# Where the last cached values, the forget rows and the first input weights are kept, in a hybrid decoder step on one core

## The reference, cut to what matters

```python
z = xn @ w_in                  # columns: conv B | C | x | q | k | v | forget logits | two merge gates
y_conv = (cb * dwconv3(cc * cx)) @ w_up_conv
# forgetting attention, 8 heads of 64; d is the running sum of log f
prompt: softmax(q.k / 8 + d_q - d_k, causal) @ v
sample: softmax over [4096 cached positions, own new positions], per sequence
    k_past = cache_k[page_table]; v_past = cache_v[page_table]; rev = sums of the cached log f
mixed = sigmoid(gA) * y_conv + sigmoid(gB) * (attn @ w_up_attn)
h = h + mixed @ w_mix_out
```

## Time and profile before

| what | value |
|---|---|
| runs | 2205.54, 2205.38, 2199.3 us; median 2205.38 us |
| profiled execution | 2202.59 us, its span in the trace 2200.9 us, mean granted TensorE clock 0.966 |
| busy: TensorE, its weight loads, VectorE, ScalarE, GpSimd | 2024.1, 1206.5, 717.2, 488.5, 260.9 us |
| chain that ended last | PE 83%, DMA 4%, DVE 4%, issue 3% |
| moved by DMA | 458.69 MB, mean 208 GB/s |

### The profile page before, as it was taken

One profiled execution on the slowest core, in us unless ns is written; L12 is line 12 of the kernel. 1 busy time (PEld: TensorE's weight loads), 2 busy tenths in 40 slices (PEclk: granted clock), 3 DMA queues, 4 the chain that ended last, 5 costly groups with the idle time before them and its releaser, 6 DMA issues.

```text
span 2200.9 us, 34422 instructions
## 1 busy us (share of the span) xinstructions
PE 2024.1 (92%) x12894; PEld 1206.5 (55%) x12894; DVE 717.2 (33%) x1652; ACT 488.5 (22%) x1058; POOL 260.9 (12%) x402
## 2 busy tenths in 40 slices
PE   7899998999969999999999989898599999999994
PEld 5677765666644665788888446654333333333331
DVE  5221223666630142333333550633511111111115
ACT  3212222544420100111110111423022222222223
POOL 1001222222223000000000000000011111111120
PEclk9999998999988999999999999999699999999997
DMA  7546777888886111310111120403799999999976
GB/s 281 179 151 230 244 268 264 273 283 275 271 283 238 48 48 52 102 48 10 58 48 63 64 79 1 144 20 145 275 374 382 383 372 371 376 374 373 370 275 242
DMA packets 205070, 458.69 MB, mean 208 GB/s; under 512 B 18721, under 2 KB 44338, under 8 KB 204778
## 3 DMA queue, kind: packets, MB, share of 16 engines
q1 hardware_dynamic: 172330, 357.96, 46.2%
q0 software_dynamic: 32576, 98.53, 13.0%
HBM read 432.51 MB, written 32.17 MB: 211 GB/s over the span
## 4 chain that ended last, share of the span: by engine, by line
PE 83%; DMA 4%; DVE 4%; issue 3%; ACT 2%; SPq 2%; DVEq 1%; POOLq 0%; ACTq 0%; POOL 0%
PE ps L1575 10%; PE ps L1057 10%; PE ps L1322 9%; PE ps L1606 5%; PE ps L1329 5%; PE ps L1586 5%; PE ps L1188 5%; PE ps L1085 5%; PE ps L1359 4%; PE ps L1615 3%; PE ps L1100 2%; PE ps L1448 2%; PE ps L1224 2%; PE ps L1199 2%; PE ps L1137 2%
## 5 line engine op out<-in xcount | busy, mean ns | idle before, releaser
L1057 PE MATMUL ps<-xnT,ring 128*128 128x352 f32 x768 | 231.3, 462 | 1.8 <-ACT xnT L727 1.8
L1575 PE MATMUL ps<-gu,xgT 128*64 128x512 f32 x1024 | 229.7, 601 | 0.9 <-ACT xgT L1936 0.9
L1057 PEld LDWEIGHTS ps<-xnT,ring 128*128 128x128 f32 x768 | 145.6, 191 | 88.8 <-issue 8.3
L2860 POOL DMA_DIRECT2D vpage<-in_cache_v x256 | 137.9, 539 | 439.9 <-issue 431.2
L1188 PE MATMUL ps<-consts,kraw 128*128 128x128 f32 x1024 | 142.6, 284 | 29.3 <-DMA kraw<-in_cache_k 17.8
L1188 PEld LDWEIGHTS ps<-consts,kraw 128*128 128x128 f32 x1024 | 115.9, 144 | 62.4 <-issue 32.0
L2211 DVE COPY kt<-ps 128x512 f32<-128x512 f32 x128 | 88.3, 691 | 183.9 <-PE ps L1188 183.2
L1575 PEld LDWEIGHTS ps<-gu,xgT 128*64 128x64 f32 x1024 | 71.3, 138 | 134.1 <-issue 131.0
L1606 PE MATMUL ps<-wd,hidT_a 128*64 128x512 f32 x512 | 116.9, 598 | 19.7 <-ACT hidT_a L1946 12.5
L2751 DVE TENSOR_TENSOR sig_a<-ps,sig_a 128x256 f32<-128x256 f32 x32 | 13.6, 425 | 326.4 <-ACT sig_a L1940 326.4
L1586 PE MATMUL ps<-gu,xgT 128*32 128x512 f32 x1024 | 115.8, 592 | 0.0
(11 more groups left out here) (429 smaller groups left out, 2862.9 us busy)
## 6 DMA issues: line engine op xcount, KB each, us to landing
kraw<-in_cache_k SPq DMA_DIRECT2D x256, 256.0 KB, 3.6
vpage<-in_cache_v POOLq DMA_DIRECT2D x256, 256.0 KB, 4.7
gu<-in_w_expert_gate SPq DMA_DIRECT2D x32, 2048.0 KB, 20.3
gu<-in_w_expert_up SPq DMA_DIRECT2D x32, 2048.0 KB, 24.8
wd<-in_w_expert_down SPq DMA_DIRECT2D x31, 2048.0 KB, 9.2
ring<-in_w_in SPq DMA_DIRECT2D x8, 1024.0 KB, 7.2
yy<-y_d SPq DMA_DIRECT2D x16, 512.0 KB, 10.1
early<-in_w_in SPq DMA_DIRECT2D x6, 1024.0 KB, 10.7
```

The costliest lines, as they stand in the source:

```text
L1057: last = nc.tensor.matmul(bank(R.bank(*tag))[:, 0:NC_], slot[:, k, f * P:(f + 1) * P], xnT[:, k, cols_of(n)], start=k == 0, stop=k == KD - 1)
L1575: last = nc.tensor.matmul(bank(0)[h * BA:(h + 1) * BA, :].rearrange("p (x n) -> p x n", x=2), src[:, k, 0:BA], weight[:, k, :, h * DE // 2 ...
L2860: pool.dma_start(vpage[n % VS][:, p, :], t["cache_v"][ds(page, 1)].rearrange("a s d -> (a s) d")).then_inc(v_in[n % VS], 16)
```

## The change

Five edits, all in the mixer's stretch but the last:

1. Values of units 54 to 63 rotate through four places: the two before and the two of `kraw`. Unit 54 waits for the last keys' turning (`kt` 62) and 55 for `kt` 63; from 56 on a unit waits for the unit that had its place (52, 53, 54, ...).
2. All loops run over 74 slots instead of 64. Units 54 to 63 are weighed one a slot, one after another, and the twelve products of `cc` stand behind them, with nothing between. The last sequence's probabilities are turned in slot 65.
3. The two pairs of places of `negk` are exchanged. Pair 0 now goes to ring place 0 and is sent in SP's step 27, after the second column block of k; pair 1 goes to the area of `xnT`, sent in step 35. Pairs 2 and 3 stay in steps 41 and 49 (`slot_after`), and the prompt's units, written by a new formula, fall into the same slots as before.
4. `cc` goes to ring place 1 and is sent first, once the scores of unit 63 are made; then `xnT`, then `cx` to place 0. All later names take the other place. `xo` (place 0) is sent ahead of `xq` (place 1), which now waits for the last product of `w_mix_out`.
5. Semaphores are merged (`wfz` with `early_k`, `halo` with `mem`), and VectorE drains before it masks a sequence's sum.

```diff
@@ -58,7 +58,7 @@
-RING_ORDER = ["cc", "cx", "cb", "xk", "xv", "g0", "g1", "g2", "g3", "mo0", "mo1", "xq", "xo"]
+RING = {"cc": 1, "cx": 0, "cb": 1, "xk": 0, "xv": 1, "g0": 0, "g1": 1, "g2": 0, "g3": 1, "mo0": 0, "mo1": 1, "xo": 0, "xq": 1}
@@ -232,7 +232,7 @@
-        negk = [[at(f"negk{d}{p}", [P, SEQ], (a_norm + 6 * 4096 if d == 0 else a_ring) + p * 4096) for p in range(2)]
+        negk = [[at(f"negk{d}{p}", [P, SEQ], (a_norm + 6 * 4096 if d == 1 else a_ring) + p * 4096) for p in range(2)]
@@ -249,8 +249,8 @@
-        VS = 2
-        vpage = [at("vpage0", [P, 4, DA], a_mem), at("vpage1", [P, 4, DA], w + 5 * 4096)]
+        VS, MORE_VS = 2, DB * SU - SU - 2
+        vpage = [at("vpage0", [P, 4, DA], a_mem), at("vpage1", [P, 4, DA], w + 5 * 4096)] + kraw
@@ -482,9 +482,11 @@
+        END = PROMPT0 + PROMPT_SLOTS
+
...
-            return [(n - PROMPT0, 0), (n - PROMPT0, 1)] if PROMPT0 <= n < PROMPT0 + NU else []
+            return [(x // 2, x % 2) for x in range(2 * NU) if PROMPT0 + x * PROMPT_SLOTS // (2 * NU) == n]
@@ -529,14 +532,10 @@
-            if n > SU and n % SU == 1:
+            if SU < n < NSU + SU and n % SU == 1:
                 add_probs(n // SU - 1)
-        R.add("dve", "so", DB - 2, banks=(6,))
-        add_probs(DB - 1)
...
-            if x == SU - 1:
-                R.add("dve", "so", DB - 1, banks=(6,))
@@ -773,40 +772,44 @@
-            return ring[RING_ORDER.index(f"g{f // 2}") % 2].rearrange("p k (x n) -> p k x n", x=2)[:, :, :, f % 2 * P:(f % 2 + 1) * P]
+            return ring[RING[f"g{f // 2}"]].rearrange("p k (x n) -> p k x n", x=2)[:, :, :, f % 2 * P:(f % 2 + 1) * P]
...
-        LOADS = {"cc": (w3(t["w_in"], O_CC), None), "cx": (w3(t["w_in"], O_CX), ("sq", NSU - 1)),
+        LOADS = {"cc": (w3(t["w_in"], O_CC), ("sq", NSU - 1)), "cx": (w3(t["w_in"], O_CX), ("po", NU - 1)),
...
-                 "xq": (w3(t["w_xq"], 0), ("m6", 0)), "xo": (w3(t["w_xo"], 0, D), ("m3", PAIRS - 1))}
+                 "xo": (w3(t["w_xo"], 0, D), ("m6", 0)), "xq": (w3(t["w_xq"], 0), ("m3", PAIRS - 1))}
...
-            n = RING_ORDER.index(name)
+            n = RING[name]
...
-            dst = ring[n % 2] if src.shape[1] == KD else ring_xo
+            dst = ring[n] if src.shape[1] == KD else ring_xo
...
-                    sp.dma_start(dst[:, :, x * 256:(x + 1) * 256], src[:, :, x]).then_inc(ring_in[n % 2], 16)
+                    sp.dma_start(dst[:, :, x * 256:(x + 1) * 256], src[:, :, x]).then_inc(ring_in[n], 16)
                 else:
-                    sp.dma_start(dst, src).then_inc(ring_in[n % 2], 16)
+                    sp.dma_start(dst, src).then_inc(ring_in[n], 16)
...
-            n = RING_ORDER.index(name)
-            pe.wait_ge(ring_in[n % 2], 16 * sum(ring_parts(x) for x in RING_ORDER[n % 2:n + 1:2]))
-            return ring[n % 2]
+            n, loaded = RING[name], 0
+            for other in RING:
+                loaded += ring_parts(other) if RING[other] == n else 0
+                if other == name:
+                    break
+            pe.wait_ge(ring_in[n], 16 * loaded)
+            return ring[n]
@@ -820,6 +823,14 @@
+
+        def value_place(n):
+
+            return n % VS if n < MORE_VS else (n - MORE_VS + VS) % 4
+
+        def values_in(n):
+
+            return sum(value_place(m) == value_place(n) for m in range(n))
@@ -866,7 +877,7 @@
-                sp.dma_start(wfz, w3(t["w_in"], O_FZ, H)).then_inc(wfz_in, 16)
+                sp.dma_start(wfz, w3(t["w_in"], O_FZ, H)).then_inc(early_k_in, 16)
@@ -916,21 +931,25 @@
-                if n == 31:
+                if n == 27:
+                    R.made(sp, "k", 1, 1)
+                    load_negk(0)
+                if n == 35:
...
-                    load_negk(0), load_negk(1)
-                if n == 41:
+                    load_negk(1)
+                if n == slot_after(PT):
                     load_negk(2)
-                if n == 49:
+                if n == slot_after(2 * PT):
...
+            ring_load(sp, "cc")
...
-            ring_load(sp, "cc"), ring_load(sp, "cx")
-            sp.dma_start(halo, t["state_conv"]).then_inc(halo_in, 16)
+            ring_load(sp, "cx")
+            sp.dma_start(halo, t["state_conv"]).then_inc(mem_in, 16)
@@ -970,11 +989,11 @@
-            ring_load(sp, "xq")
+            ring_load(sp, "xo")
...
-            ring_load(sp, "xo")
+            ring_load(sp, "xq")
@@ -1216,13 +1234,13 @@
-                pe.wait_ge(v_in[n % VS], 64 * (n // VS + 1))
+                pe.wait_ge(v_in[value_place(n)], 64 * values_in(n) + 64)
...
-                                            vpage[n % VS][:, j, :], start=u == 0, stop=u == SU - 1 and j > 0)
+                                            vpage[value_place(n)][:, j, :], start=u == 0, stop=u == SU - 1 and j > 0)
@@ -1240,12 +1258,13 @@
-            for n in range(NSU):
-                sample_scores(n)
+            for n in range(NSU + LAG):
+                if n < NSU:
+                    sample_scores(n)
...
-                if n == PROMPT0 + NU:
+                if n == END:
@@ -1272,16 +1291,12 @@
-                if n > SU and n % SU == 1:
+                if SU < n < NSU + SU and n % SU == 1:
                     turn_sample_probs(n // SU - 1)
-            weigh_pages(NSU - LAG), weigh_pages(NSU - LAG + 1)
-            turn_sample_probs(DB - 1)
...
-                if x < SU:
-                    weigh_pages((DB - 1) * SU + x)
@@ -1296,7 +1311,7 @@
-            pe.wait_ge(halo_in, 16)
+            pe.wait_ge(mem_in, 32)
@@ -2235,12 +2249,13 @@
-            for n in range(NSU):
-                join_scores(n)
+            for n in range(NSU + LAG):
+                if n < NSU:
+                    join_scores(n)
...
-                if n == PROMPT0 + NU:
+                if n == END:
@@ -2283,11 +2297,6 @@
-            R.made(dve, "so", DB - 1)
-            nc.vector.tensor_tensor(masked, bank(6), consts[:, C_DIAG:C_DIAG + DA], ALU.mult)
-            dve.drain()
-            nc.vector.tensor_reduce(own[:, DB - 1, :], masked.rearrange("p (h d) -> p d h", h=H), AX, ALU.add
-                                    ).then_inc(R.by["dve"], 1)
@@ -2854,11 +2863,13 @@
-                if n >= VS:
-                    pool.wait_ge(v_used, n - VS + 1)
+                if values_in(n):
+                    pool.wait_ge(v_used, max(m for m in range(n) if value_place(m) == value_place(n)) + 1)
+                elif n >= VS:
+                    R.made(pool, "kt", NSU - 2 + n - MORE_VS, KC - 1)
                 for p, page in enumerate(unit_pages(pool, n)):
-                    pool.dma_start(vpage[n % VS][:, p, :], t["cache_v"][ds(page, 1)].rearrange("a s d -> (a s) d")
-                                   ).then_inc(v_in[n % VS], 16)
+                    pool.dma_start(vpage[value_place(n)][:, p, :], t["cache_v"][ds(page, 1)].rearrange("a s d -> (a s) d")
+                                   ).then_inc(v_in[value_place(n)], 16)
```

More of the change, by code:

```diff
@@ L381, in build_program @@
         x_in = [sem(f"x_in{i}") for i in range(TILES)]
-        mem_in, halo_in, wfz_in = sem("mem_in"), sem("halo_in"), sem("wfz_in")
+        mem_in = sem("mem_in")
         ring_in = [sem(f"ring_in{s}") for s in range(2)]
@@ L399, in build_program @@
         k_in = [sem(f"k_in{s}") for s in range(2)]
-        v_in = [sem(f"v_in{s}") for s in range(VS)]
+        v_in = [sem(f"v_in{s}") for s in range(4)]
         rev_in = [sem(f"rev_in{p}") for p in range(2)]
@@ L463, in build_program @@
                  + [("k", f, n) for f, n in REST])
-        PROMPT0, KOUT0 = 29, 30
+        PROMPT0, PROMPT_SLOTS, KOUT0 = 29, 32, 30
         def items(n):
@@ L501, in build_program @@
                 add_keys(n, c)
-        for n in range(NSU):
-            R.add("dve", "sq", n, banks=(5,))
+        for n in range(NSU + LAG):
+            if n < NSU:
+                R.add("dve", "sq", n, banks=(5,))
             if n + 2 < NSU:
@@ L884, in load_rev, with slot_after @@
                                  .unsqueeze(1).to_broadcast([H, DS, SU * PAGE])).then_inc(rev_in[b % 2], 16)
+            def slot_after(k):
+                return PROMPT0 + 2 * k * PROMPT_SLOTS // (2 * NU) + 4
             def load_negk(hp):
@@ L1117, in _ @@
                     n_mix.pe_turn(pe, x)
-            pe.wait_ge(early_k_in, 16)
+            pe.wait_ge(early_k_in, 32)
             for f in range(KC):
                 early_product("k", f, COLS - 1, early_k[:, :, f * P:(f + 1) * P])
-            pe.wait_ge(wfz_in, 16)
             R.read(pe, "nmix", 0, 0), R.read(pe, "nmix", 0, 1)
@@ L1364, in mixed_rows @@
                 return mixT[:, 0:HK, i * P:(i + 1) * P] if low else mixT[:, HK:KD, i * P:(i + 1) * P]
-            out0, out1 = ring_slot(pe, "mo0"), ring[RING_ORDER.index("mo1") % 2]
+            out0, out1 = ring_slot(pe, "mo0"), ring[RING["mo1"]]
             for i in range(PAIRS):
@@ L1818, in _ @@
                     copy_key_rows(n - KOUT0)
-                if n >= SU and n % SU == 0:
```

(9 more changed lines are left out.)

## The result

The changed kernel takes 2214.51 us (median of 7 runs, 2210.39 to 2218.95), the one before 2205.38 us in the 7 runs beside them. The ratio is 1.0051, 95% interval 1.0038 to 1.0063: 11 us slower by it, 9 by the medians. The profiled execution took 2217.07 us, its span is 2215.4 us, 14.5 longer than the span before.

A forecast was written before the change was run, and what follows sets the result against it. TensorE was taken to set the pace, with holes in slot 29 and at the end of the cached pages. -10 + 19 = +9 us gave 2211.6 against 2202.59, 2213 with a share of the median's offset; range 2199 to 2223.

The forecast's parts named there:

- POOL's pace: End of cached pages: POOL issues units 54 to 63 at 4.55 to 4.88 us each, the last by 687.2 or 690.5.
- Forget rows: Slot 29: pair 0 sent four slots ahead removes the `negk` wait; 10 us gained, ends 5 and 13.
- keys 31 land at 350.5: Slot 29: keys 31, the next late load, there at about 350.5 instead of 353.01, a page landing 3.6 us after issue.
- The price at keys 27: Step 27: 1 MB of forget rows put among keys TensorE already awaits costs 0 to 3 us, taken as 0.5.
- only exchanged: Slot 29 rival: the wait passes to keys 31 and successors, 3 us gained instead of 10; 2219 to 2221, chance 0.05.
- Landing of unit 63 at 696: End of cached pages: last values land between 690.5 and 700, taken as 696, where POOL's and DMA's limits meet.
- the case of half for each: End-of-values rival: each queue gets half of DMA, last unit lands at 700 to 701; 2217 to 2219, chance 0.12.
- Twelve bare products: After the last weighing, `cc` products run with nothing between; about 57 us, `cx` at 761 against 742.50, loss taken as 19.
- Nothing for ring places: Ring places and merged semaphores: later loads such as `xq` stay hidden, by 11 us for `xq`; no cost.
- Faster: End-of-values rival: page-number reading shrinks or overlaps, 2.8 us a unit, last lands at about 674; 2190 to 2193, chance 0.13.
- the point of decision: Landing of unit 63: before about 687 the kernel is faster than before, after it slower.
- The two sides cancel: End-of-values rival: last values land at 690.5, +13, with -11.5 in slot 29; net +1.5, 2204 to 2207, chance 0.22.

The follow-up runs named there:

- e5: Changed kernel with all values, units 54 to 63 too, in the two old places: 2230.22 us, ratio 1.0130 to the kernel before.
- e7: e6 with units 54 to 63 loaded from fixed pages, POOL reading no page numbers for them: 2205.60 us, ratio 1.0014 to the kernel before.
- e1: Kernel before with only the forget rows' exchange: 2193.81 us, ratio 0.9957 to the kernel before.
- e3: Kernel before with only the four places for units 54 to 63, weighings still between the `cc` products: 2206.54 us, ratio 1.0010.
- e4: Kernel before with the forget rows' exchange and the four places, weighings still between the `cc` products: 2198.41 us, ratio 0.9976.
- e9: e4 with SP sending the first third of `xnT`, then `cc`, the other two thirds, then `cx`: 2189.71 us, ratio 0.9937 to the kernel before.
- e10: e1 (two places) with SP sending `cc` after the first third of `xnT`: 2196.65 us, ratio 0.9971 to the kernel before.
- e6: Changed kernel with `cx` and `mem` sent only after the last value is weighed: 2211.53 us, ratio 1.0044 to the kernel before.

## Why the prediction was right

The forecast was 2213 us, 9 slower; measured are 2214.5, 9 to 11 slower (the two profiled executions are 14.5 apart). The sum was -10 and +19, and the mechanism, POOL's pace and full DMA ahead of bare products, is what the traces and e5 to e7 show. Where luck had a part it is said below.

1. *Forget rows, -10 (5 to 13).* e1 gives -9.5 (6 to 13). In the trace slot 29 gained 8.6, not 10.8, and 3.6 were lost elsewhere ahead of the end part, so that this one trace has -5.0 to the mark. The mark moves by up to 10 us between traces of kernels that agree until then; by the means of the ten with the rows exchanged (629.8) and the three without (639.0) it comes 9 us sooner. With +20.7 and the -1.3 behind `halo` that makes +10, as the runs have it. The step that was off: I let keys 31 land at 350.5, by the median of 3.6 us for a page. Slot 29 starts 1.1 us later here, and keys 31 came 4.80 us behind its start (3.88 in e1), 5.63 before, where I took 3.1. POOL issues 1 MB of values beside them (347.10 to 349.39), and from 340 to 356 keys took 5.0 us to land and values 5.7 in the median, not 3.6. I had left these values out; that they are the cause is argued, as no run takes them away. The price at keys 27, taken as 0.5 us, measured 0.8, and -0.5 in e1. The "only exchanged" rival is refuted by e1.
2. *POOL's pace, 4.55 to 4.88 us, last issue at 690.5 against a unit 53 issued at 639.36.* In the changed kernel everything there is 5.04 us sooner, and the last issue ended at 685.5, which is 690.6 in the forecast's frame: ten units of 4.55 us and 3.4 us of stops amid units 54, 58 and 59. Here luck had a part: the forecast came to 690.5 by the slower pace, 4.88, and at the measured pace it would have been 687.2; the stops, whose reason is open, made up for it. That this pace was read from two rows that looked unimportant was the step that settled the sign.
3. *Landing of unit 63 at 696.* It is weighed at 693.34, in that frame 698.4. The mis-sized term is the way from issue to landing: 7.8 us instead of 5.5, since DMA was full to the end. DMA in the changed kernel, 640 to 700 (each figure in the first line is the rate in 1.5 us):

```profile
GB/s 354 281 352 400 400 391 387 375 388 378 369 387 375 376 384 384 370 387 360 385 376 372 388 387 377 403 376 389 382 388 385 386 386 399 350 96 3 0 11 0
...
q0 software_dynamic: 3220, 10.53, 46.6%
q1 hardware_dynamic: 5421, 9.43, 44.3%
```

   The rate stays near 380 GB/s until about 692 and the stretch moves 20 MB, as the count of bytes said (21 MB from 641 to 696). POOL's queue (q0) carried 10.53 MB to SP's (q1) 9.43 MB, at 46.6% and 44.3% of the engines' time. By the Trainium skill (DMA: Bandwidth & Descriptors, "Queues, rings and completion order") the turns go by packet. The prediction read this as half of DMA for each queue, which it is only for packets of one length: here 3220 packets of some 3.3 KB stand against 5421 of some 1.7 KB, so neither the packets nor their lengths are equal, and no run here shows the rule of turns. The near equality of time is no rule either: in e7, from 640 to 680, it was 58.8% to 41.0%. In bytes values had the larger part (0.53), so the last unit came between my forecast and the case of half for each.
4. *Twelve bare products and what lies around them.* From 693.34 to the first product of `cx`, at 758.25, are 64.9 us; I had 65.0. Sum of the end part: +20.7 instead of the 19 taken.
5. *Nothing for ring places, `xq`, `wfz`, `halo`.* Behind `halo` the two traces differ by 1.3 us in favour of the changed one.
6. *The rivals.* "Faster" needed POOL to read its page numbers for free. e7 does that, with `cx` and `mem` out of the way besides: its unit 63 is weighed 50.2 us after the mark, 686.5 in the forecast's frame, and it is level with before (1.0014), as the point of decision (687) had it. But a unit took 3.9 us even then, not the 2.8 of bytes alone, since `xnT` had 41% of DMA's time, so the 674 of that case was not reached. "The two sides cancel" needed the last values 5 to 6 us sooner than the 696 of the forecast; they came 2 later.

What the forecast did not have: the four places alone, in the old order, cost 3 us of the end part rather than bring some, because the landing of `cc` then becomes the wait (e3, e4). It did not enter the sum, since in the changed order nothing needs them before 697.

What stays open: whether the values issued beside keys 31 are what holds these, why POOL stops amid units 54, 58 and 59, and what moves the mark by up to 10 us from one trace to another of kernels that agree until then (625.1 to 634.9 in ten traces with the rows exchanged, 636.3 to 640.4 in three without).

## What to carry to other kernels

Work that stands between waits is what hides them: before it is moved, count how often the queue that feeds the waits can deliver by itself, issue cost of its engine and bytes under full DMA both, and whether anything else can run meanwhile. More places for a stream pay only if what shares the DMA engines with it is not needed first; the order in which SP sent `xnT` and `cc` decided whether four places cost 2 us of the end part (e4 against e1) or brought 7.6 (e9 against e10). And a load sent when its place came free, rather than late with its neighbour, gained more than any other single edit.

## What the runs showed of the hardware

- Reading four page numbers into registers costs POOL 2.25 us and issuing four DMAs of 256 KB 2.29 us, nearly without spread (in e6 too); with fixed pages four issues take 2.12 us and the gap is gone (e7).
- With DMA full at 380 GB/s a page of values landed 6.6 to 6.7 us after issue in the median (changed kernel, 640 to 700), and 10.5 to 11.2 where more of them were under way (e7, 640 to 680); over the whole kernel before the median of values is 4.7 and of keys 3.6.
- Behind a wait of 2.02 us TensorE's next group ran at the upper clock (1.06 us at 634.33), behind 4.83 us at the lower (1.94 us at 641.11). At 661.54, behind work without a wait from 653.23 to 660.6, it was back at the upper (1.07 us), and behind the next wait of 3.56 us at the lower again, until the `cc` products. In e7, with shorter waits (0.8 to 3.2 us), all groups from 635 to 679 were at the lower.
